# Tile 1's row products spread over the other tiles' gate products, branches and norms

## What is computed

```python
    y = jax.nn.sigmoid(ga) * (o_rec @ w_branch_rec) + jax.nn.sigmoid(gb) * (o_att @ w_branch_att)
    x = layer_norm(DEEPNORM_ALPHA * x + g1 * (y @ w_out), ln1_g, ln1_b)
    h2 = x * (1.0 + sc2) + sh2
    x = layer_norm(DEEPNORM_ALPHA * x + g2 * peer_mixer(h2, ...), ln2_g, ln2_b)

def peer_mixer(...):
    ...  # per token: 8 heads choose 16 of 16384 experts each, 128 in all, with a softmax gate
    def block(args):
        xb, eb, gb = args
        a = jax.nn.gelu(jnp.einsum('td,thkd->thk', xb, u_tab[eb]), approximate=False)
        return jnp.einsum('thk,thkd->td', gb * a, v_tab[eb])
```

## Time and profile before

| | |
|---|---|
| median of 3 runs | 5514.78 us |
| the profiled execution: its time, its span | 5514.83 us, 5512.9 us |
| busy in the span: PE, DVE, POOL, ACT | 81%, 62%, 39%, 27% |
| mean DMA traffic | 311 GB/s |
| layer 0: first mix (start), first sum (start), last sum (start) | 1321.88, 1576.28, 1719.40 us |
| layer 1: first mix (start), first sum (start) | 4066.96, 4320.44 us |

### The profile page before, as it was taken

One profiled execution on the slowest core, in us unless ns is written; L12 is line 12 of the kernel. 1 busy time (PEld: TensorE's weight loads), 2 busy tenths in 40 slices (PEclk: granted clock), 3 DMA queues, 4 the chain that ended last, 5 costly groups with the idle time before them and its releaser, 6 DMA issues. The chain is left out here.

```text
span 5512.9 us, 63669 instructions
## 1 busy us (share of the span) xinstructions
PE 4464.5 (81%) x18920; PEld 2395.5 (43%) x18920; DVE 3395.8 (62%) x6888; ACT 1508.3 (27%) x3912; POOL 2126.0 (39%) x1814
## 2 busy tenths in 40 slices
PE   7889997889595777777787899978895957777776
PEld 6556653446352323222265566535462523232222
DVE  2357776427778766754533677764187887677545
ACT  2112223520011333333321123135100113334333
POOL 0002125613656454455500021255036564445554
PEclk8999998999797999999999999989997989999999
DMA  7655447976989999999957454578679899999998
GB/s 271 254 199 182 141 163 263 335 255 251 372 319 341 420 420 417 416 421 418 404 215 271 173 180 143 195 263 325 238 274 364 327 342 420 420 413 416 420 419 345
DMA packets 299169, 1712.36 MB, mean 311 GB/s; under 512 B 34384, under 2 KB 44240, under 8 KB 178768
## 3 DMA queue, kind: packets, MB, share of 16 engines
q0 software_dynamic: 258048, 1342.29, 62.3%
q1 hardware_dynamic: 23712, 338.18, 16.2%
q10 hardware_dynamic: 17072, 27.83, 1.6%
HBM read 1694.53 MB, written 5.24 MB: 308 GB/s over the span
## 5 line engine op out<-in xcount | busy, mean ns | idle before, releaser
L430 POOL DMA_INDIRECT arena<-in_peer_uv,eidx x856 | 949.4, 1109 | 1200.6 <-POOLq L429 1004.5
L970 PE MATMUL banks<-arena 128*128 128x512 f32 x896 | 496.1, 636 | 238.2 <-PEq L1594 236.9
L2315 DVE SCALAR_TENSOR_TENSOR arena<-arena 128x1024 f32<-128x1024 f32 x384 | 470.7, 1226 | 350.4 <-DMA arena<-in_peer_uv,eidx 340.3
L482 POOL DMA_INDIRECT arena<-in_peer_uv,eidx x384 | 494.3, 1287 | 481.2 <-POOLq L481 458.4
L943 PE MATMUL banks<-ring,arena 128*128 128x512 f32 x864 | 384.8, 600 | 114.1 <-PEq L925 114.1
L972 PE MATMUL banks<-arena 128*128 128x512 f32 x896 | 472.1, 609 | 0.0
L534 ACT ACTIVATE arena<-arena 128x1 f32<-128x1 f32 (+1 forms) x770 | 156.2, 203 | 1039.4 <-ACTq L533 1039.2
L545 ACT ACTIVATE arena<-ident,arena 128x128 f32<-128x128 f32 x832 | 333.6, 401 | 301.0 <-ACTq L544 298.1
L970 PEld LDWEIGHTS banks<-arena 128*128 128x128 f32 x896 | 153.3, 195 | 549.0 <-issue 548.1
L1990 DVE SCALAR_TENSOR_TENSOR arena<-arena 128x1024 f32<-128x1024 f32 x256 | 308.4, 1224 | 99.6 <-DMA arena<-in_peer_uv,eidx 80.4
L2325 DVE SCALAR_TENSOR_TENSOR arena<-arena 128x1024 f32<-128x1024 f32 x256 | 307.0, 1225 | 98.8 <-DMA arena<-in_peer_uv,eidx 91.9
(11 more groups left out here) (319 smaller groups left out, 7573.5 us busy)
## 6 DMA issues: line engine op xcount, KB each, us to landing
ring<-in_wblk SPq DMA_DIRECT2D x160, 2048.0 KB, 8.5
arena<-in_peer_uv,eidx POOLq DMA_INDIRECT x1240, 7.2
arena<-arena ACTq DMA_DIRECT2D x64, 128.0 KB, 6.2
arena<-in_lnrows ACTq DMA_DIRECT2D x6, 1024.0 KB, 9.0
ring<-in_peer_uv,eidx POOLq DMA_INDIRECT x360, 6.6
arena<-in_sk ACTq DMA_DIRECT2D x4, 1024.0 KB, 7.6
hT<-in_peer_uv,eidx POOLq DMA_INDIRECT x192, 14.1
x<-in_x_sample ACTq DMA_DIRECT2D x1, 2048.0 KB, 28.5
```

The costliest lines, as they stand in the source:

```text
L430: nc.gpsimd.indirect_dma_start(row_buf[j], None, ins["peer_uv"], bass.IndirectOffsetOnAxis(ap=eidx[:, n, c:c + 1].bitcast(U32), axis=0)).t ...
L482: nc.gpsimd.indirect_dma_start(gslot[j], None, ins["peer_uv"].rearrange("(e h) d -> e (h d)", h=2), bass.IndirectOffsetOnAxis(ap=eidx[:, n ...
L970: nc.tensor.matmul(banks[:, b, :], diag[n], row[:, 0:CB], start=start, stop=stop, skip_group_check=True).then_inc(diag_used, 1)
L2315: V.scalar_tensor_tensor(u, u, 1.0, h2[:, t - 2, :], ALU.mult, ALU.mult, accum_out=av[:, r:r + 1])
```

## The change

It does four things, all in the per-layer part described above.

1. DVE's dots: 13 stand between mix 1 and mix 2, and 13 before each further mix up to mix 7 (`MIX_DOTS`; 78 by then). Ahead of the branches of tiles 2, 3 and 4 stand 10, 8 and 8 (`NORM_DOTS`), behind each `norm_stats` one more; 21 follow the last norm into h2.
2. Tile 1's activation comes in two halves of 64 columns. The first is released when 65 dots are done, and stands on ACT behind the eighth sigmoid; the second stands behind the scores of the first query block.
3. The product with the gates comes in halves too (`weigh_tile`): the first ahead of 64 sums, the second behind them.
4. The memset of `acc` stands ahead of these, and x's three norms stand behind the first 64 sums. ACT's wait for them (`x_normed`) moves from the first score block behind the last.

```diff
--- before.py
+++ after.py
@@ -43,6 +43,7 @@
 TURNS = SLOTS // ROWS
 DIAGS = 4
 DIRECT = 96
+MIX_DOTS, NORM_DOTS = 13, (10, 8, 8)
 PAIRS = QH // 2
 STEPS = PAIRS * LT
 
@@ -857,11 +858,10 @@
                         nc.scalar.activation(sg[f][:, c * GRP:(c + 1) * GRP], banks[:, 4 * f + c, 0:GRP], ACT.Sigmoid
                                              ).then_inc(bank_free[4 * f + c], 1)
                     act.drain().then_inc(sg_ready[f], 1)
+                gelu(0, SLOTS // 2).then_inc(gelu_ready, 1)
                 for t in range(2, NT):
                     square_root(1)
                 for t in range(2, NT):
-                    if t == NT - 1:
-                        gelu(0, SLOTS).then_inc(gelu_ready, 1)
                     turned(hT[:, :, (t - 1) * P:t * P], 2 * (t % 2))
 
                 def query_part(u):
@@ -880,12 +880,13 @@
                     for u in range(4):
                         query_part(u)
                         if u:
-                            if n == 0 and u == 1:
-                                act.wait_ge(x_normed, 1)
-                                act.sem_inc(x_normed, -1)
                             score_part(4 * n + u - 1, u - 1)
                     score_part(4 * n + 3, 3)
+                    if n == 0:
+                        gelu(SLOTS // 2, SLOTS).then_inc(gelu_ready, 1)
                 act.drain().then_inc(stage_ready, 1)
+                act.wait_ge(x_normed, 1)
+                act.sem_inc(x_normed, -1)
                 copy_out(bc2, 0)
                 load_norm(ln2, 2, ln2_full)
                 act.wait_ge(wv_ready, 1)
@@ -2345,16 +2346,32 @@
                     V.tensor_tensor(yT[:, n, :], sg[f][:, 0:GRP], sg[f][:, GRP:2 * GRP], ALU.add).then_inc(sg_free[f], 1)
                     dve.drain().then_inc(y_ready, 1)
 
+                def weigh_tile(half):
+
+                    c = slice(half * SLOTS // 2, (half + 1) * SLOTS // 2)
+                    dve.wait_ge(gelu_ready, 1)
+                    dve.sem_inc(gelu_ready, -1)
+                    V.tensor_tensor(wv[:, c], av[:, c], gates[0][:, c], ALU.mult)
+                    dve.drain()
+
                 mix(0)
-                for n in range(1, KD):
+                mix(1)
+                at = 0
+                for n in range(2, KD):
+                    one_dots(at, at + MIX_DOTS)
+                    at += MIX_DOTS
+                    if at - MIX_DOTS < SLOTS // 2 <= at:
+                        dve.drain().then_inc(dots_ready, 1)
                     mix(n)
-                    one_dots(SLOTS * (n - 1) // (KD - 1), SLOTS * n // (KD - 1))
-                dve.drain().then_inc(dots_ready, 1)
                 gain, base, scale, shift = one_tile.ln1[:, 0], one_tile.ln1[:, 1], one_tile.bc[:, 1], one_tile.bc[:, 2]
                 for t in range(2, NT):
+                    one_dots(at, at + NORM_DOTS[t - 2])
+                    at += NORM_DOTS[t - 2]
                     for h in range(2):
                         add_branch(t, h, 2 * (t - 2) + h, one_tile.bc, tmp_grp)
                     norm_stats(t)
+                    one_dots(at, at + 1)
+                    at += 1
                     xt, dst = x[:, t, :], h2[:, t - 2, :]
                     dve.wait_ge(std_ready, 1)
                     dve.sem_inc(std_ready, -1)
@@ -2362,18 +2379,20 @@
                     dve.drain()
                     norm_rows(dst, xt, small[:, 128 + 2 * t:129 + 2 * t], small[:, 144 + t:145 + t], scale, shift
                               ).then_inc(h2_ready, 1)
-                dve.wait_ge(gelu_ready, 1)
-                dve.sem_inc(gelu_ready, -1)
-                V.tensor_tensor(wv, av, gates[0], ALU.mult).then_inc(wv_ready, 1)
+                one_dots(at, SLOTS)
+                dve.drain().then_inc(dots_ready, 1)
+                dve.wait_ge(acc_free, 1)
+                dve.sem_inc(acc_free, -1)
+                V.memset(acc, 0.0)
+                weigh_tile(0)
+                one_sum(0, SLOTS // 2)
+                weigh_tile(1)
+                dve.drain().then_inc(wv_ready, 1)
                 for t in range(2, NT):
                     norm_rows(x[:, t, :], x[:, t, :], small[:, 128 + 2 * t:129 + 2 * t], small[:, 144 + t:145 + t],
                               gain, base)
                 dve.drain().then_inc(x_normed, 1)
-                dve.wait_ge(acc_free, 1)
-                dve.sem_inc(acc_free, -1)
-                V.memset(acc, 0.0)
-                dve.drain()
-                one_sum(0, DIRECT)
+                one_sum(SLOTS // 2, DIRECT)
                 dve.drain().then_inc(acc_done, 1)
                 choose(one_tile, gates[1])
                 V.tensor_scalar(eid[:, 0].bitcast(U32), e1, layer_base[:], None, ALU.add).then_inc(idx_ready, 1)
```

## The result

The changed kernel takes 5484.26 us (median of 4 runs, 5479.78 to 5487.76) against 5517.52 for the kernel before on the same chip (median of 4). The ratio is 0.9937, with a 95% interval of 0.9920 to 0.9954. A second measurement of the same kernel, made beside the experiments, gave 5488.6 us and 0.9952 (0.9938 to 0.9965). The forecast was 5485.8 us.

A forecast was written before the change was run, and what follows sets the result against it. Neither DVE nor DMA is full; they take turns waiting. Parts A to D end layer 0's sums at 1706.2 instead of 1720.7: 14.5 us, 29 over two layers, 5514.8 - 29 = 5485.8 us; 8 in 10 within 5455 to 5504.

The forecast's parts named there:

- turn-taking of dots and norms: Layer 0 before: DVE waits 46.1 us for rows in its dots, POOL 33.8 us for a buffer during branches and norms.
- Part A: From the first mix to mix 7's end: five rows (6.4 us) and one block (5.1 us) more, ending at 1464.0.
- The lower bound: Earliest case for the stretch to mix 7's end: DVE follows PE at 1452, 10 us less.
- Part B: Branches and norms of tiles 2 to 4 with 29 dots: 33.4 + 24.9 + 2 = 60.3 us, to 1524.3.
- rival 3: `w_out` becomes the bound at the lower clock: some 82 us in place of 44, 5546 us in all; chance 0.04.
- Part C: The 21 dots behind the last norm into h2: 28 us, until the last row lands; sums start at 1553.7.
- Part D: The 96 sums with x's norms in the middle: 152.5 us, 11.9 of it waits for rows, ending at 1706.2.
- Rival 1: The 37 us stretch of branches and norms with DMA share 0.52 is filled entirely: 5442 to 5464 us; chance 0.20.
- Rival 2: Waits for rows move into the sums, which take 12 us more: gain 2.5 per layer, 5510 us; chance 0.12.

The follow-up runs named there:

- e2: The kernel before with the dots alone moved as in the change; activation whole, x's norms ahead of the sums: 5490.4 us, 0.9954.
- e1: The kernel before with only x's three norms moved behind the first 64 sums, and ACT's wait behind the last score block: 5515.2 us, 0.9996.
- e4: The changed kernel with a drain behind every dot of tile 1: 5482.04 us, 0.9934 of the kernel before.
- e5: The kernel before with a drain behind each dot of tile 1: 5498.93 us, 0.9971.
- e3: The changed kernel with 18 dots between mixes and 6, 5 and 4 ahead of the branches: 5512.77 us, 0.9993 of the kernel before.
- e9: The changed kernel with branch dots cut finer (8, 5, 5 ahead; 4, 3, 3 between each branch's halves): 5480.37 us, 0.9941 of the kernel before.
- e10: The changed kernel with the finer cut of e9 and a drain behind each dot: 5482.02 us, 0.9936 of the kernel before.

## Why the prediction was right

**Right, and shown.** That the turn-taking of dots and norms costs and the moved dots earn it back: e2 has the gain, e1 has none, and e4 against e5 shows some 20 us of it without slow issues. That `acc_done` carries it to the end: what follows it is as long as before. The size: 14.5 us a layer forecast, 14.3 and 15.8 measured, 12.8 and 14.6 in the second execution.

**Part A.** Mix 7 was forecast at 140.3 us behind the first mix and came at 140.0 and 138.4. The sum of five rows and a block on top of a row of the trace was enough: the row, mix 5 before, held 4 us of what slow issues cost (e5 has it at 124.5 in place of 128.8 us behind the first mix), while in the changed kernel they cost mix 7 7.2 us (e4), so the fit within 0.3 us is finer than the sum was. e3 confirms the link to the rhythm (188.1 with 18 dots). PE was sooner than the prediction had it: product 7 was done 121.7 us behind the first mix and not near 1452, 130 us behind it. The lower bound was set too high by this; the forecast didn't rest on it, since rows and blocks bound part A.

**Part B.** Forecast to end at 202.4, measured 205.1 and 201.9. The wait for PE's second bank was 4.7 and 2.6 us where 2 was forecast. Ten dots and half a branch took 13.1 us, as forecast (1459.23 to 1472.31); but `w_out` began 0.65 us behind the mix, and its first bank took 9.95 us in layer 0 and 8.9 in layer 1, the later ones 6.87, where I had 7.3 for each. The granted clock was 0.50 from 1459 to 1463 and 1.00 from 1466 on, behind 20.71 us of idling: the first bank ran in part at the lower of the two levels. This is rival 3 in small. The square root was hidden but for 0.43 us.

**Part C: the time right, the mechanism wrong.** I had 28 us, from eight full buffers emptied at 1.15 us a dot while POOL sets off a row each 2.29. It took 26.5 us, from 1522.57 to the last dot's end at 1549.06, but no issue in it took 1.99: the first of 20 took 1.14, the others 0.93 to 1.00, and from the third dot on DVE followed them, nearly all 1.27 to 1.28 us apart. The buffers were not full when part C began. The slow issues had come sooner, in part B, 11 of 30, where I had none, taking it that DMA had time to spare there. The two errors nearly cancel, because 21 rows at 1.27 us are 26.7, near the 28 that came from another sum. That the time agrees is luck.

**Part D.** Forecast 152.5 us with 11.9 of waits; measured 151.4 and 147.1 (with 132.5 of sums and 8.1 of norms and gates: 10.8 and 6.5 of waits). The norms in the middle neither helped nor hurt: before it was 11.9 and 6.8 in the two layers (144.4 and 139.3 less 132.5).

**The rivals.** Rival 1, the hole filled entirely, falls: part B runs at 0.85. Rival 2, waits that move into the sums, falls. e1 and e3 look like its cases, since they start the sums 7 to 11 us sooner and end them no sooner, but that is the 8 us of norms within them: less these and 132.5 of sums, the rest is 11.1 and 6.7 us in e1 and 12.3 and 7.6 in e3, hardly different from the 11.9 and 6.8 before. Rival 3, `w_out` as the bound, falls: 44.45 us with 20.71 of idling ahead, against 44.0 with 45.07.

**The rule on the shared port.** The prediction set the Trainium skill's inference (SBUF — State Buffer, "Who interferes with whom"), that descriptor writing isn't held up by an instruction with two inputs in SBUF, against 1.99 us in the trace. The Trainium skill draws it for `tensor_tensor`. The runs decide for the trace: with a drain behind each dot (e4) 29 issues over 1.9 us became 1, and issues end 0.81 us behind a norm (1484.43) or a mix's `tensor_tensor` (1369.94) as they do behind a dot. It is not the accumulator's read, which stands behind the dots alone. That a second input in SBUF is what holds the issue fits all rows, products with a bank as an input included; that it is the port which the Trainium skill names is not shown by them.

**What stays open.** The measurement has 0.09 to 0.17% on each side of a ratio, so which of e4, e9, e10 and the changed kernel is best can't be said. That e5 gains 17 us by a drain while e4 gains nothing on top of the change fits the view that both pay for the same late rows, but it was not taken further. Nor was the change's rhythm tried without the spreading over the norms.

## What to carry to other kernels

When a gather feeds one engine through few buffers, count for each stretch the rows and blocks that DMA must bring and the work that its partners have, and give the feeding engine so many rows that the three come out equal: here 13 rows and a block (21.6 us) against a product of 21.3. Five rows more a product or two less both lost the whole gain (14 in place of 13, both with drains, made no difference that shows). The spacing of back-to-back work on the consumer can slow the producer's issues, so a small pause in it may cost nothing: compare when the issue begins with when the consumer's instruction ends. And a start that is 7 us sooner is worth nothing where the work behind it grew by as much: follow each gain to the instruction that ends the stretch.

## What was not expected of the hardware

- An indirect DMA issue on POOL that begins while DVE runs an instruction with both tensor inputs in SBUF ends 0.81 us behind that instruction's end (410 of 411 in e4, counted as above); otherwise it takes 0.94 us. Dots back to back (start to start 1.15 us) thus stretch it to 1.99 us, with a drain between them (1.33 us) it takes 1.02. On the kernel before this one line is worth 17 us, 0.29%.
- Of the schedule and not of the hardware, but as little expected: 18, 13 and 11 dots between mixes, with the others moved behind mix 7, give 5513, 5484 to 5489 and 5514 us.
